# Reordering the first two groups of gathered rows in a sparse expert layer

## The reference

```python
q = (hf @ w_q).reshape(T, PEER_HEADS, 2, PEER_DQ // 2)
s = jnp.einsum('thpd,hpnd->thpn', q, sub_keys)
sc, idx = lax.top_k(s, PEER_TOPK)
cand = sc[:, :, 0, :, None] + sc[:, :, 1, None, :]          # 16 x 16 sums per head
top_sc, pos = lax.top_k(cand, PEER_TOPK)
eidx = jnp.take_along_axis(cidx, pos, axis=-1)
gate = jax.nn.softmax(top_sc, axis=-1)
act = jax.nn.gelu(jnp.einsum('thkd,td->thk', u_tab[eb], hb), approximate=False)
return jnp.einsum('thk,thkd->td', gb * act, v_tab[eb])
```

## Time and profile before

| | us |
|---|---|
| median of 3 runs | 1605.81 |
| lowest and highest | 1605.28, 1606.15 |
| the profiled execution | 1605.89 |
| its span, first instruction to last | 1603.8 |
| PE busy | 1484.7 |
| DVE busy | 1056.0 |
| POOL busy | 570.2 |
| ACT busy | 551.5 |

### The profile page before, as it was taken

How to read it: one execution, slowest core, us unless ns; L and a number is a source line. 1 busy time by engine, 2 the same in 40 slices (tenths; PEclk the granted TensorE clock), 3 DMA queues, 4 the chain that set the end, 5 groups by cost and what they waited for, 6 DMA issues and landing times.

```text
span 1603.8 us, 22836 instructions
## 1 busy us (share of the span) xinstructions
PE 1484.7 (93%) x8300; PEld 1140.7 (71%) x8300; DVE 1056.0 (66%) x2176; ACT 551.5 (34%) x1145; POOL 570.2 (36%) x382
## 2 busy tenths in 40 slices
PE   8999999999999999999999998898989897788777
PEld 7999997767999999998989995444444343333233
DVE  6655385755743328998984658785858585858456
ACT  6434353454444436443116243221212121212113
POOL 2555437120244441001001324455544444544341
PEclk9999999999999999999989999999999999989999
DMA  9888958993999997999956849999999999999996
GB/s 365 317 319 330 349 211 336 321 331 138 392 372 369 370 383 286 368 399 343 360 207 234 352 197 364 426 426 427 427 427 427 427 426 427 427 427 426 427 428 274
DMA packets 99670, 571.91 MB, mean 357 GB/s; under 512 B 11520, under 2 KB 11648, under 8 KB 50176
## 3 DMA queue, kind: packets, MB, share of 16 engines
q1 hardware_dynamic: 61056, 298.15, 49.9%
q0 software_dynamic: 37376, 268.47, 39.9%
q10 hardware_dynamic: 1152, 4.16, 0.7%
HBM read 569.67 MB, written 135.27 MB: 440 GB/s over the span
## 4 chain that ended last, share of the span: by engine, by line
PE 59%; DMA 23%; DVE 11%; issue 3%; POOL 3%; ACT 2%; ACTq 0%; POOLq 0%; DVEq 0%
DMA arena<-pairs,eidx 17%; PE ps L2697 10%; PE ps L2087 8%; PE ps L2085 8%; PE ps L2086 8%; DMA ring<-pairs,eidx 4%; DVE arena L1613 3%; PE ps L2174 2%; PE ps L2172 2%; PE ps L2173 2%; PE ps L2425 2%; POOL arena L799 2%; PE ps L2476 1%; PE ps L2590 1%; PE ps L2662 1%
## 5 line engine op out<-in xcount | busy, mean ns | idle before, releaser
L2697 PE MATMUL ps<-arena 128*128 128x512 f32 x912 | 430.5, 626 | 83.9 <-ACT arena L1232 83.9
L2697 PEld LDWEIGHTS ps<-arena 128*128 128x128 f32 x912 | 177.5, 199 | 321.7 <-issue 205.4
L1939 DVE CUSTOM_DVE_ANT_0 arena<-arena 128x1024 f32<-128x1024 f32 x228 | 275.5, 1223 | 160.5 <-DMA arena<-pairs,eidx 160.4
L799 POOL DMA_INDIRECT arena<-pairs,eidx x228 | 272.5, 1195 | 285.3 <-PE ps L2697 244.5
L734 POOL TENSOR_TENSOR w_lo<-ring,w_hi 128x1024 fp32r<-128x1024 f32 x76 | 208.1, 2740 | 258.9 <-DVE w_lo L1285 175.0
L2085 PE MATMUL ps<-u_hi,w_hi 128*128 128x256 f32 (+1 forms) x912 | 259.5, 285 | 3.6 <-POOL w_lo L734 1.5
L2087 PE MATMUL ps<-u_hi,w_lo 128*128 128x256 f32 (+1 forms) x912 | 259.6, 285 | 0.0
L2086 PE MATMUL ps<-u_lo,w_hi 128*128 128x256 f32 (+1 forms) x912 | 259.1, 284 | 0.0
L817 ACT ACTIVATE w_hi<-ring 128x1024 fp32r<-128x1024 f32 x188 | 197.7, 1056 | 150.1 <-PE ps L2174 71.2
L2085 PEld LDWEIGHTS ps<-u_hi,w_hi 128*128 128x128 f32 x912 | 172.1, 189 | 5.3 <-issue 2.3
L2087 PEld LDWEIGHTS ps<-u_hi,w_lo 128*128 128x128 f32 x912 | 172.3, 189 | 0.0
(11 more groups left out here) (390 smaller groups left out, 2464.6 us busy)
## 6 DMA issues: line engine op xcount, KB each, us to landing
ring<-in_stream SPq DMA_DIRECT2D x121, 1024.0 KB, 7.2
pairs<-in_peer_u SPq DMA_DIRECT2D x128, 512.0 KB, 7.6
pairs<-in_peer_v SPq DMA_DIRECT2D x128, 512.0 KB, 8.9
arena<-in_ada SPq DMA_DIRECT2D x32, 768.0 KB, 6.6
arena<-in_stream SPq DMA_DIRECT2D x8, 1024.0 KB, 10.4
arena<-pairs,eidx POOLq DMA_INDIRECT x228, 18.0
h<-in_x_t SPq DMA_DIRECT2D x2, 544.0 KB, 4.7
ring<-in_stream SPq DMA_DIRECT2D x2, 512.0 KB, 7.2
```

The lines of the kernel that those rows point to most:

```text
L799: pool.indirect_dma_start(slot_of(n), None, pairs, bass.IndirectOffsetOnAxis(ap=eidx[:, n:n + 1], axis=0)).then_inc(landing(n)[0], 16)
L1939: dve.tensor_tensor_reduce(row, row, hf[:, n % HEAD_ROWS // TOPK, :], 1.0, 0.0, ALU.mult, ALU.add, dots[:, n % HEAD_ROWS:n % HEAD_ROWS + 1 ...
L2697: mm = pe.matmul(ps[:, Y_BANKS[j // TOPK] + half, :], diag[:, n % DIAGS, :], slot_of(n)[:, D + half * 512:D + half * 512 + 512], start=(hd ...
```

## The change

No instruction is added or dropped; calls are moved on three engines, around groups 0 to 2.

- **DVE**: `dot(2)` and `dot(3)`, `gate_made(0, [0])` now come ahead of tile 1's `first_query(1)` (line 1765), and `weights(0)` ahead of the eight products that make tile 1's tokens (line 2009). Before, `weights(0)` stood inside `choose_halves` of tile 1.
- **ACT**: group 0's Gelu and diagonals come ahead of tile 1's `first_query`, `first_scores` and `shifted`. The copies of head 1's query and scores and `first_gate_exp(1)`, which before stood behind group 0 and (the last) behind group 1, all stand behind group 1, `first_gate_exp(1)` last.
- **PE**: `first_scores(1)` stands between row 1 and row 2 instead of ahead of group 0; the two turns of tile 1's tokens stand behind group 0 instead of ahead of it; `all_scores(1)` stands behind group 1 instead of ahead of it.

```diff
@@ ACT
-            first_query(1)
-            first_scores(1)
-            for k in range(KT):
-                shifted(1, k)
...
                 if g == 0:
+                    first_query(1)
+                    first_scores(1)
+                    for k in range(KT):
+                        shifted(1, k)
                     for n in range(2, 2 * TT):
                         tok_copy(n)
+                if g == 1:
                     for e in range(2):
                         half_head(1, e)
                     score_copy(1)
-                if g == 1:
                     first_gate_exp(1)
@@ DVE
-            dot(0)
-            dot(1)
+            for n in range(GROUP):
+                dot(n)
+            gate_made(0, [0])
             first_query(1)
+            weights(0)
...
-                if g in (0, 2):
-                    gate_made(0, [g // 2])
+                if g == 2:
+                    gate_made(0, [1])
@@ PE
             def weigh_rows(g):
                 for n in range(GROUPS[g].start, GROUPS[g].stop):
+                    if n == 2:
+                        first_scores(1)
...
-            first_scores(1)
             next_query(0, 1)
-            pe.wait_ge(u_done, 6 * KT)
-            tok_turn(2)
-            tok_turn(3)
             pe.wait_ge(tok_ev, 2)
             for g in range(len(GROUPS)):
                 if g == 1:
+                    pe.wait_ge(u_done, 6 * KT)
+                    tok_turn(2)
+                    tok_turn(3)
                     for e in range(2):
                         next_query(1, e)
+                if g == 2:
                     all_scores(1)
```

More of the change, by code:

```diff
@@ L2021, in _ @@
                 for n in range(group.start, group.stop):
-                    if n > 1:
+                    if n >= GROUP:
                         dot(n)
-                    if n == group.start and g and n <= SINGLE and not parts_behind(g - 1):
+                    if n == group.start and g > 1 and n <= SINGLE and not parts_behind(g - 1):
                         weights(g - 1)
@@ L2037, in _ @@
                         scaled(0)
-                if g in (0, 2):
-                    gate_made(0, [g // 2])
+                if g == 2:
+                    gate_made(0, [1])
                 for i, (part, of_head, tiles) in enumerate(parts_behind(g)):
-                    part(of_head, tiles, (lambda: weights(g)) if i == 0 else None)
+                    part(of_head, tiles, (lambda: weights(g)) if i == 0 and g else None)
                 if hd < HEADS - 1 and at == len(parts) + (2 if hd == 0 else 0):
```

## The result

The changed kernel takes 1607.26 us (median of 22 runs, 1605.44 to 1608.56); the kernel before, run beside it, 1604.65 (22 runs, 1603.14 to 1606.66). The ratio is 1.0014, interval 1.0008 to 1.0019: slower by 1.3 to 3.1 us. That is under the 0.2% called "the same" in the prediction, but clear of zero, and on the other side from the forecast gain of 0.35 us. Two executions of kernels further down, one of 2956.59 us (copies early) and one of 3770.0 (both waits filled), are recorded as slow and left out of every median and ratio.

A forecast was written before the change was run, and what follows sets the result against it. The prediction took queued gathers at DMA's 427 GB/s as the bound. Losses of 5.65 us plus 1.24 for a refill, 6.9 against 7.25, gained 0.35: from 1605.89 to 1605.54, less 0.08 over the median, 1605.5 us; 8-in-10 range 1603.0 to 1608.6.

The forecast's parts named there:

- What bounds the kernel: Gathers queue at 427 GB/s, 2.456 us each; only DMA time lost early counts, 7.25 us, at most 6.0 winnable.
- Group 0: First refill: weights(0) 1.55 us earlier, gather of row 8 at 966.6 to 967.2 instead of 968.76, closing DMA's bubble.
- what is late for it: Tile 1's choose_halves at 969.1 instead of 964.25, dots 4 to 7 3.9 us later, yet weights(1) 978.15 instead of 979.10.
- the clock in group 1: Second refill: if TensorE stays at 2.4 GHz, group 1 takes 7.1 us and row 13's gather goes out at 980.9.
- the refill: Ahead of row 17's data: refilling DMA's empty queue costs 1.24 us as at the start, bounds 0 to 1.24.
- main sum: DMA up to row 17: 5.65 us lost plus 1.24, 6.9 against 7.25, a gain of 0.35 us.
- Rival 1: TensorE's clock falls at group 1 or 2: one fall 1607.2 us, chance 0.28; both 1608.9, chance 0.10.
- Group 2 is where it is given back: Third refill: gate's exponent done at 989.1 instead of 982.1, gather of row 17 at 994.85 instead of 994.02.
- Rival 2: Gains at rows 8 and 13 kept, group 2 starting by about 989.6: DMA loses 2.6 us, 1601.2 us; chance 0.07.
- Rival 3: Change doesn't reach row 8, dot 3 or POOL's issue being late: forecast or up to 1 us more, 1606.5; chance 0.08.

The follow-up runs named there:

- copies early: Changed kernel with head 1's query copies ahead of group 1's Gelu on ACT and its scores ahead of group 1 on PE; 1602.93 us, ratio to before 0.9983.
- both waits filled: Changed kernel with two unused matmuls in PE's wait ahead of group 1 and two more ahead of group 2; 1605.83 us, ratio to before 1.0004.
- gate first: Changed kernel, but ACT takes the exponent of tile 1's gate ahead of the copy of head 1's scores; 1605.69 us, ratio to before 1.0004.
- first half alone: Changed kernel, but head 1's scores again ahead of group 1 on PE and its copies behind group 0 on ACT; 1603.67 us, ratio to before 0.9992.
- weights first: The copies early kernel, with weights(2) on DVE right behind the gate instead of inside choose_halves of head 1; 1602.00 us, ratio to before 0.9980.

## Why the prediction was wrong

**What bounds the kernel** was right. In all ten profiles DMA's loss in the first 90 us and the time to the end move together: end less loss is 649.1 to 649.9 us, whatever was changed.

**Group 0 and what is late for it** were right nearly to the digit. Counted from row 0, row 8 was forecast for 19.2 to 19.8 and came at 19.6; choose_halves of tile 1 for 21.65 and came at 21.4; weights(1) for 30.7 and came at 30.4; dot 3 waited 0.83 us for row 3 (0.9 forecast).

**Two terms failed: the clock in group 1 and the refill.** The first: "If the clock stays at 2.4 GHz, the gather of row 13 goes out at 980.9". It didn't stay. Group 1 took 8.83 us, not 7.1, and row 13 went out at 34.8 us from row 0 where that sentence means 33.45. I had the row that says so (8.83 us after a wait of 1.41), forecast a longer wait, 2.2 us, at the same place, and still put the fall in a rival with 0.28. The changed kernel's two profiles and the one with the gate first, all with this wait of 2.21 us, show 8.83 us; with only 0.5 to 0.6 us of wait left it was 7.13 in four kernels. The row of before should have weighed more in the main sum, though it wasn't proof: first half alone waited 1.42 us at the same place and kept 2.4 GHz. Both waits filled says what the step was worth: 0.9 to 1.2 us to the end.

Rival 1, one fall, gives 1607.2, and 1607.26 was measured, but that closeness is luck. Its sum starts from 1605.81, the median of 3 runs of the kernel before, and 22 runs give 1604.65. As a difference rival 1 says 1.4 us slower, at the low end of the 1.3 to 3.1 measured.

**Group 2 is where it is given back** was right as a mechanism: the exponent behind the score copy, the gate made at 43.5 us from row 0 (42.15 forecast, 43.85 with the clock's fall), row 17 at 48.8 (47.4, and 49.1 with the fall). Gate first shows that this hold-up costs time, with the clock's fall left as it was, and both waits filled against first half alone shows it with the clock held in both. What I took for ACT's table load was right too. The exponent started 1.30 us behind the load's start and the load 0.01 us behind the score copy. The 2.66 us of the Trainium skill, "ScalarE: Activation LUTs", section "What ACT_TABLE_LOAD costs", which include a drain, aren't seen in this trace.

**The refill was mis-sized, and it gave the forecast its sign.** I took 1.24 us for filling the empty queue, from the first window, and as the most that it could be. Loss less (position of row 17 less 41.75 us) is 1.4 to 2.2 us in the nine other profiles, 1.9 in the changed kernel's first. It is 2.4 in the kernel before. So I set a worked-out loss of 6.9 us against a measured one of 7.25; worked out the same way, the kernel before loses 6.1. With 1.9 in place of 1.24 the sum is 7.55 us, 0.3 more than before, and the change is slower even with the clock held. Both waits filled, which is that case, ended 0.4 us later than the kernel before, though its ratio of 1.0004 is too near 1 for the times to say it. The sum's own row 17, 0.83 us later than before, already pointed that way. The forecast's 6.9 us, plus 1.7 for the clock and 0.65 for the refill, less 0.35 by which group 2 was ready sooner, make 8.9, the loss that the windows show; the 0.65 is what was left over, so this sum checks the other terms only.

**Rivals.** Rival 1 (one fall) is what happened. Rival 2 (gains kept) needed another order on ACT; the kernel with weights first comes part of the way there. Rival 3 was out: row 8 was reached. Its detail was right, row 7's issue (at 958.17 us) stretched to 1.91 us beside dot 2 and cost nothing.

What stays open: whether the clock falls in group 1 in every execution of the changed kernel. Only profiled ones show it, and filling both waits changed the ratio from 1.0015 to 1.0004 with intervals that overlap. What decides a fall isn't settled either: TensorE's clock held after 2.29 us ahead of group 2 and not after 2.21 ahead of group 1, and it held after 1.42 us in first half alone and not after 1.41 in the kernel before. Nor is it known why the kernel before has the highest of the refills.

## What to carry to other kernels

When a bandwidth-bound stage starts with a few buffers, look at each refill in turn and forecast the last late one: work won at the first refills is kept only if the last empty moment of the queue comes earlier. Before an instruction is put behind another in a queue, ask what the one ahead of it waits for; here a 0.2 us exponent stood behind an 8.4 us wait. Two reorderings that each gain can lose together if one delays what the other has been made to depend on, so time the halves apart; a state of the clock that the trace shows at a place has to be priced in the main sum when the wait ahead of that place grows; and a small difference is worked out for both kernels by the same sum, never as a sum against a measurement.

## What the runs showed of the hardware

**The clock's fall moves.** With the wait ahead of group 1 filled, about as much (1.6 us) was lost one group later, behind a wait of 2.30 us: granted clock 0.77 over that group. Filling one wait with useless matmuls therefore bought nothing; filling both bought 0.9 to 1.2 us to the end. The wait's length alone doesn't tell: the clock fell after 1.41, 2.21 and 2.30 us and held after 1.42 and 2.29.

**A gather's issue waits for the dot product that is running.** POOL's instruction takes 0.93 to 1.03 us in every issue with no dot beside it, in all ten profiles from 940 to 1060 us. One that begins while a dot runs ends 0.80 to 0.83 us after that dot does, in all but four of some 170: row 7 of the changed kernel began at 958.17 us and ended at 960.08, dot 2 having ended at 959.27. Issues of 1.4 to 2.0 us come of that, and single ones reach 2.2 to 2.55. One that begins as the dot does can keep its 0.94 us (row 17 of the kernel before, at 994.02). The Trainium skill, "SBUF — State Buffer", section "SBUF: two separate sides", has a DVE instruction with two SBUF inputs and a GpSimd one that reads SBUF exclude each other. The trace agrees where the dot is first, with 1.91 us against 0.94; where the issue is first it doesn't show the dot held up, 1.26 us against 1.22. At rows 13 to 20 this stretch lies in the refill, and may be part of the 0.65 us by which it was mis-sized; that was not tried.

**Row 17 tells the time.** Over ten profiles with row 17 from 43.5 to 48.8 us, the end came 608.8 to 610.2 us after row 17's gather, the kernel before among them with 609.8.
